# Opening of a transformer-layer kernel on one TensorE core: x in six 96-token chunks, first products by quarters

## The reference, cut to what matters

```python
u = rms_norm(h, g_mix_pre[i])                    # h is x; y = x * rsqrt(mean(x*x) + eps) * g
qa, ka, va, qb, kb, vb = jnp.split(u @ w, IN_SPLITS, axis=-1)
# then: two attention mixers per head, gates, merge, output projection,
# h + rms_norm(...), FFN with relu squared, and a gated per-layer embedding
```

## Time and profile before

| | |
|---|---|
| median of 3 runs | 1178.62 us (1177.7 to 1179.76) |
| the profiled execution: its time / its span | 1179.02 us / 1177.3 us |
| TensorE busy, share of the span | 98% |
| weight loads busy | 93% |
| VectorE, ScalarE, GpSimd busy | 41%, 36%, 43% |
| mean granted TensorE clock | 0.991 |
| chain that ended last: TensorE's share | 91% |

### The profile page before, as it was taken

One profiled execution on the slowest core, in us unless ns is written; L12 is line 12 of the kernel. 1 busy time (PEld: TensorE's weight loads), 2 busy tenths in 40 slices (PEclk: granted clock), 3 DMA queues, 4 the chain that ended last, 5 costly groups with the idle time before them and its releaser, 6 DMA issues.

```text
span 1177.3 us, 23187 instructions
## 1 busy us (share of the span) xinstructions
PE 1151.8 (98%) x8374; PEld 1094.8 (93%) x8374; DVE 487.3 (41%) x910; ACT 425.9 (36%) x905; POOL 508.6 (43%) x424
## 2 busy tenths in 40 slices
PE   8999999999999999999999989999999999999897
PEld 7888888888888889999999989999999999999897
DVE  2655555656534341112352276215413421541665
ACT  5344444454443444332233253213212221222342
POOL 3545544453444333333445454534444444444541
PEclk8999999999999999999999999999999999999899
DMA  5233422222232222232222212322222222222122
GB/s 158 82 92 93 137 75 82 89 89 69 84 93 75 92 75 63 81 101 80 81 84 86 63 54 72 99 81 82 87 81 80 80 86 84 80 80 81 53 72 81
DMA packets 167338, 98.82 MB, mean 84 GB/s; under 512 B 8801, under 2 KB 162650, under 8 KB 167282
## 3 DMA queue, kind: packets, MB, share of 16 engines
q1 hardware_dynamic: 159538, 82.05, 24.0%
q0 software_dynamic: 7744, 16.02, 4.2%
HBM read 88.57 MB, written 11.02 MB: 85 GB/s over the span
## 4 chain that ended last, share of the span: by engine, by line
PE 91%; DVE 5%; ACT 1%; issue 1%; POOL 0%; DVEq 0%; ACTq 0%
PE proj L1353 75%; PE turn_out L1525 3%; PE score L1443 3%; PE turn_out L1504 2%; PE turn_out L1520 1%; DVE wide L1219 1%; PE turn_out L1389 1%; PE turn_out L1475 1%; PE score L1450 1%; DVE hT L1248 1%; PE score L1381 1%; ACT prob L679 1%; DVE prob L1043 1%; PE turn_out L1537 1%; DVE act_lo L1237 1%
## 5 line engine op out<-in xcount | busy, mean ns | idle before, releaser
L463 POOL TENSOR_TENSOR w_lo<-w_raw,w_hi 128x512 fp32r<-128x512 f32 x292 | 394.4, 1354 | 587.8 <-ACT w_hi L627 587.6
L1353 PE MATMUL proj<-act_hi,w_hi 128*128 128x288 f32 x1600 | 362.5, 308 | 8.8 <-DVE act_lo L1237 3.5
L1353 PE MATMUL proj<-act_lo,w_hi 128*128 128x288 f32 x1600 | 344.4, 297 | 0.0
L1353 PE MATMUL proj<-act_hi,w_lo 128*128 128x288 f32 x1600 | 343.6, 297 | 0.0
L627 ACT ACTIVATE w_hi<-w_raw 128x512 fp32r<-128x512 f32 x292 | 182.3, 628 | 380.9 <-PE proj L1353 379.2
L1353 PEld LDWEIGHTS proj<-act_hi,w_hi 128*128 128x128 f32 x1600 | 255.0, 190 | 29.8 <-issue 16.6
L1353 PEld LDWEIGHTS proj<-act_lo,w_hi 128*128 128x128 f32 x1600 | 259.0, 190 | 0.0
L1353 PEld LDWEIGHTS proj<-act_hi,w_lo 128*128 128x128 f32 x1600 | 258.8, 190 | 0.0
L1353 PE MATMUL proj<-mid_hi,w_hi 128*128 128x288 f32 x640 | 137.3, 296 | 0.0
L1353 PE MATMUL proj<-mid_hi,w_lo 128*128 128x288 f32 x640 | 137.3, 295 | 0.0
L1353 PE MATMUL proj<-mid_lo,w_hi 128*128 128x288 f32 x640 | 137.3, 295 | 0.0
(11 more groups left out here) (207 smaller groups left out, 1110.7 us busy)
## 6 DMA issues: line engine op xcount, KB each, us to landing
w_raw<-w_in SPq DMA_DIRECT2D x72, 256.0 KB, 3.0
w_raw<-w_up SPq DMA_DIRECT2D x64, 256.0 KB, 2.8
w_raw<-w_down SPq DMA_DIRECT2D x64, 256.0 KB, 2.8
w_raw<-w_gate SPq DMA_DIRECT2D x32, 256.0 KB, 2.7
w_raw<-w_branch_b SPq DMA_DIRECT2D x16, 256.0 KB, 2.9
w_raw<-w_out SPq DMA_DIRECT2D x16, 256.0 KB, 2.8
w_raw<-w_ple_gate SPq DMA_DIRECT2D x16, 256.0 KB, 2.9
out<-k_tm POOLq DMA_DIRECT2D x12, 256.0 KB, 3.8
```

The costliest lines, as they stand in the source:

```text
L463: pool.tensor_tensor(w_lo[:, slot], w_raw[:, slot], w_hi[:, slot].bitcast(F32), ALU.subtract).then_inc(lo_done, 1)
L1353: last = pe.matmul(out[:, h], w[:, slot, at], x[:, k, HALF * h:HALF * h + HALF], start=(k == 0 and s == 0), stop=(k == blocks - 1 and s == 2))
```

## The change

Six chunks of 96 tokens (XC, XR) instead of 4 x 128 + 64: chunks 0 to 2 are token half 0, chunks 3 to 5 are half 1 (the last is 32 prompt and 64 sample tokens, by two DMAs). SP issues weight pieces 0 and 1 between the two triples of chunks. The 16 half-block tiles (X_TILES) are taken in four groups of four: features 0-511 of half 0, features 0-511 of half 1, then features 512-1023 of half 0 and of half 1. They rotate through four banks (score and turn_out, two halves each); proj is no longer used for x. Each tile takes three transposes, one ScalarE split (L637 after), one VectorE subtraction (L952 after) and one VectorE copy to hT (L955 after), all on 288 columns and reading the bank. Products go by groups: projection 0 for the group, then projection 1. Idle matmuls before the first products go from 16 + 40 to 8 + 4 + 16 (the last 16 on half of the array's rows each). Squares, means and roots are regrouped: one mean and one root over all six chunks instead of five each.

```diff
-        X_EARLY = 4
-        def x_bank(j):
-            return (score, turn_out, proj[0], proj[1])[j if j < X_EARLY else j % 2]
+        GROUP = KB // 2
+        X_TILES = [(GROUP * (g // 2) + j, g % 2) for g in range(4) for j in range(GROUP)]
+        def x_bank(i):
+            return (score[:, 0:HALF], score[:, 512:512 + HALF],
+                    turn_out[:, 0:HALF], turn_out[:, 512:512 + HALF])[i % GROUP]
...
-            for t in range(QB - 1):
-                sp.dma_start(x_tm[:, t], xp[P * t:P * t + P]).then_inc(x_loaded[t], 16)
-            sp.dma_start(x_tm[0:SMP, QB - 1], xs_d).then_inc(x_loaded[QB - 1], 16)
-            piece(Count(0), k_half(w_in[0], 0, b_cols[0]))
+            for c in range(XC // 2):
+                sp.dma_start(x_tm[:, c], xp[XR * c:XR * c + XR]).then_inc(x_loaded[c], 16)
+            for j in range(2):
+                piece(Count(j), k_half(w_in[0], 0, b_cols[j]))
+            for c in range(XC // 2, XC - 1):
+                sp.dma_start(x_tm[:, c], xp[XR * c:XR * c + XR]).then_inc(x_loaded[c], 16)
+            sp.dma_start(x_tm[0:XR - SMP, XC - 1], xp[SEQ - (XR - SMP):SEQ]).then_inc(x_loaded[XC - 1], 16)
+            sp.dma_start(x_tm[XR - SMP:XR, XC - 1], xs_d).then_inc(x_loaded[XC - 1], 16)
+            for j in range(2):
+                piece(Count(2 + j), k_half(w_in[0], 1, b_cols[j]))
...
-            for t in range(QB - 1):
-                root_x(t)
-            for p in range(2):
+            for p in range(RING):
                 lo_part(Count(p))
...
-            root_x(QB - 1)
...
+            pool.wait_ge(x_mean, 1)
+            pool.tensor_tensor(r_x, sq_x, neg_half[0:XR, 0:1].broadcast_to([XR, XC]), ALU.pow).then_inc(x_rooted, 1)
             for n in range(6):
                 lo_part(Count(RING + n))
...
+            def split_x(i):
+                j, h = X_TILES[i]
+                act.wait_ge(x_turned, i + 1)
+                act.activation(act_hi[:, j, HALF * h:HALF * h + HALF], x_bank(i), ACT.Copy,
+                               scale=gcol[:, G_PRE + j:G_PRE + j + 1]).then_inc(g_hi, 1)
...
+            for i, (j, h) in enumerate(X_TILES):
+                c = slice(HALF * h, HALF * h + HALF)
+                dve.wait_ge(g_hi, i + 1)
+                dve.scalar_tensor_tensor(out=act_lo[:, j, c], in0=x_bank(i), scalar=gcol[:, G_PRE + j:G_PRE + j + 1],
+                                         in1=act_hi[:, j, c].bitcast(F32), op0=ALU.mult, op1=ALU.subtract
                                              ).then_inc(g_split, 1)
+                dve.tensor_copy(hT[:, j, c], x_bank(i)).then_inc(x_kept, 1)
...
             pe.wait_ge(idle_ready, 1)
-            keep_warm(16, 512, 512)
+            keep_warm(8, 512)
...
+            for c in range(3):
+                pe.wait_ge(x_loaded[c], 16)
+                for i in range(GROUP):
+                    turn_x(i, (c,))
+                if c < 2:
+                    keep_warm(2, P)
+                else:
+                    keep_warm_halves(8, 512)
...
+            def first_products(m, group):
+                kh, h = group // 2, group % 2
+                p = 2 * kh + m
+                if h == 0:
+                    pe.wait_ge(lo_done, p + 1)
+                for j in range(GROUP):
+                    k, at = GROUP * kh + j, slice(P * j, P * j + P)
+                    pe.wait_ge(g_split, GROUP * group + j + 1)
...
+            for group in range(4):
+                for j in first_products(0, group):
+                    pass
+                if group == 0:
+                    for c in range(3):
+                        pe.wait_ge(x_loaded[3 + c], 32 if c == 2 else 16)
+                        for i in range(GROUP):
+                            turn_x(GROUP + i, (c,))
+                if group == 3:
...
+                for j in first_products(1, group):
+                    if 0 < group < 3:
+                        turn_x(GROUP * (group + 1) + j, (0, 1, 2))
```

More of the change, by code:

```diff
@@ L666, in _ @@
+            split_x(3)
+            square_x(2)
+            square_x(3)
+            for i in range(4, 8):
+                split_x(i)
+            hi_part(Count(2))
+            hi_part(Count(3))
+            square_x(4)
+            for i in range(8, 12):
+                split_x(i)
+            square_x(5)
+            hi_part(Count(RING))
+            for i in range(12, 16):
+                split_x(i)
+            hi_part(Count(RING + 1))
             act.wait_ge(lam_ready, 1)
@@ L1365, in unit_steps, with two_tasks @@
                     yield from k_steps(u * 3 + (PJ_IN + n), u * 6 + 2 * n, act_hi, act_lo)
-            def two_tasks(n, p, ready, before, between=None):
+            def two_tasks(n, p, ready, before):
                 tasks = [k_steps(Count(n + j), Count(p + j), act_hi, act_lo, apart=2) for j in range(2)]
@@ L1373, in two_tasks @@
                         next(task)
-                    if between:
-                        between(k)
             def row_matmuls(r, valid):
@@ L1383, in row_matmuls, with keep_warm, keep_warm_halves @@
                 return last
-            def keep_warm(count, first, n):
+            def keep_warm(count, n):
                 for _ in range(count):
-                    pe.matmul(turn_out[:, first:first + n], idle_w[:, :], idle_x[:, 0:n], start=True, stop=True)
+                    pe.matmul(proj[1][:, 0:n], idle_w[:, :], idle_x[:, 0:n], start=True, stop=True)
+            def keep_warm_halves(count, apart):
+                for _ in range(count):
+                    for r in range(2):
+                        rows_ = slice(64 * r, 64 * r + 64)
+                        pe.matmul(proj[1][:, apart * r:apart * r + HALF], idle_w[rows_, :], idle_x[rows_, 0:HALF],
+                                  start=True, stop=True)
@@ new lines, in turn_x @@
+            def turn_x(i, chunks):
+                j, h = X_TILES[i]
+                if i >= GROUP:
+                    pe.wait_ge(x_kept, i - GROUP + 1)
+                for c in chunks:
+                    last = pe.transpose(x_bank(i)[:, XR * c:XR * c + XR], x_tm[:, 3 * h + c, P * j:P * j + P],
+                                        ident[0:XR, 0:XR])
+                if chunks[-1] == 2:
+                    last.then_inc(x_turned, 1)
+            for c in range(3):
[6 more added lines that the diff above has]
+                    keep_warm_halves(8, 512)
@@ new lines, in _ @@
+            pe.wait_ge(gains_ready, 1)
+            def first_products(m, group):
[6 more added lines that the diff above has]
+                    pe.wait_ge(g_split, GROUP * group + j + 1)
+                    for s, (w, x) in enumerate(((w_hi, act_hi), (w_lo, act_hi), (w_hi, act_lo))):
+                        last = pe.matmul(acc[m][:, h], w[:, p, at], x[:, k, HALF * h:HALF * h + HALF],
+                                         start=(k == 0 and s == 0), stop=(k == KB - 1 and s == 2))
+                    if h == 1 and j == GROUP - 1:
+                        last.then_inc(w_used, 1)
+                    yield j
@@ L1426, in in_between @@
-                    row_matmuls(r_x, rows).then_inc(x_row_ready, 1)
-            for b in range(2):
-                pe.wait_ge(x_kept[b], 1)
-            two_tasks(PJ_IN, 0, g_split, 0, between=in_between)
+                    pe.wait_ge(x_rooted, 1)
+                    for c in range(XC):
+                        at = 512 * (c // 3) + XR * (c % 3)
+                        last = pe.matmul(score[:, at:at + XR], r_x[:, c:c + 1].broadcast_to([XR, P]),
+                                         ident[0:XR, 0:XR], start=True, stop=True)
```

117 lines of the change are left out of this document (30 added, 87 removed).

## The result

| | before | after |
|---|---|---|
| median of 10 runs each | 1178.61 us (1176.07 to 1179.76) | 1171.67 us (1168.29 to 1175.57) |
| ratio | | 0.9947 (95%: 0.9934 to 0.9959) |
| profiled execution: time, span, mean clock | 1179.02, 1177.3, 0.991 | 1171.4, 1169.8, 0.993 |
| first product | 17.65 | 11.53 |
| third projection | 39.42 | 32.46 |

The kernel became 0.5% faster: 6.9 us in the medians, 7.5 in the two spans, of which 6.96 had been won by the third projection. What stands behind it is 0.6 shorter. The forecast was 1170.9; but its two terms came out otherwise: the start 6.1 earlier instead of 7.4, and the way to the third projection 20.9 instead of 21.5.

What follows compares the result with a forecast made beforehand. TensorE, busy 98% of the span, bounds the kernel, so only the opening can yield time: -7.4 - 3.7 + 2.8 + 0.6 = -7.7 us takes the profiled 1179.0 to 1171.3, median 1170.9; range 1168.0 to 1174.5.

Steps and rivals of the forecast that it cites:

- 7.4 earlier: Opening: the first product comes at 10.2 us instead of 17.65.
- chunk 2 (1.18 MB) at 6.7 to 7.1: Opening, data stream: the last x chunk of half 0 is there at 6.7 to 7.1 us.
- The bound of 11.4: Latest first product, 11.4 us, if weight piece 0 lands only when 2.1 MB had landed before (9.39).
- at 0: Opening: TensorE's wait for half 1's x chunks, asked for at 11.9 us, costed at 0; 0.8 kept for the range.
- +2.8: First product to third projection: 16 more transposes between add 1.8 us, five more product-transpose changes at 0.2 add 1.0.
- -3.7: First product to third projection: low clock (2.8 us) and waits for w_lo and VectorE's first projection result removed.
- rival 1: Opening: the clock falls after all, costing 1.4 to 2.8 us, time 1172.3 to 1173.7; chance 0.27.
- +0.6: Groups 1 to 3: new TensorE waits for VectorE's tiles, 0.1 to 1.4 us in sum, taken as 0.6.
- rival 2: VectorE sets the pace: subtraction 0.8 us, a tile 1.3, waits 5.2 us instead of 0.6, time 1175.5; chance 0.08.
- The rule on small tiles: VectorE and ScalarE: fixed latency per instruction, tiles of 512 elements or more advised; by it 288-column tiles are wrong.
- Rival 3: Opening: the weights land late, first product at 11.4 us, time 1172.1; chance 0.10.
- rivals 4 and 5: Lead lost behind 39 us, 1178.6, chance 0.03; clock at 1.2 GHz until the third projection, 1185.2, chance 0.04.

Runs made afterwards that it cites:

- Run 9: Changed kernel with x chunks 0 to 4 loaded over all 128 partitions, a third more bytes, only 96 rows of each used: 1172.19 us, ratio 0.9954.
- run 11: Changed kernel with VectorE's hT copies behind each group's four subtractions and more idle matmuls, second run of this combination: 1170.67 us, ratio 0.994.
- Run 10: Changed kernel with copies last, more idle matmuls and x cut as 128, 128, 32 and 128, 96, 64 tokens: 1176.2 us, ratio 0.9984.
- run 1: The changed kernel measured again, unchanged: 1172.64 us, ratio 0.9957 to the kernel before.
- run 3: Changed kernel with VectorE's four copies to hT moved behind each group's four subtractions: 1170.04 us, ratio 0.9936.
- run 12: Kernel before with three x blocks transposed ahead instead of four, and 12 idle matmuls filling the stand before the first product: 1179.09 us, ratio 1.0022.
- run 2: Changed kernel with each 96-token chunk of x loaded by two transfers, of 64 and 32 rows: 1173.98 us, ratio 0.9964.
- run 4: Changed kernel with all 28 idle matmuls of the opening removed: 1171.49 us, ratio 0.9944.

## Why the prediction was right, and where its terms were off

- *The start, "7.4 earlier"*: 6.1. The rule that TensorE, ScalarE and GpSimd follow the bytes held, link for link. The term that was mis-sized is "chunk 2 (1.18 MB) at 6.7 to 7.1": it took the stream's 0.4 MB per us of before, whose chunks cover 128 partitions, for chunks of 96. Measured were 219 to 315 GB/s from 3 to 9 us, and 8.26. Run 9 shows why. The bound of 11.4 was passed by 0.13.
- *Half 1's chunks "at 0"*: the 0.62 us of waiting at 14.82, inside the 0.8 kept for the range, and from the same cause.
- *"+2.8"* for 16 more transposes and five changes: too much. A round of three products and three transposes costs 0.68 in run 11's chain, against 0.95 by the forecast's prices (3 x 0.139 + 3 x 0.11 + 0.2). Eight rounds make 2.2 us less, and two terms of the price were off. A transpose of 96 tokens takes 0.08 instead of 0.11: that is the gain that the forecast had foreseen but left unpriced (at most 1.0), some 0.7 in these rounds. The larger part, some 1.5, is the 0.2 for a change from products to transposes and back, of which next to nothing is left (3 x 0.139 + 3 x 0.083 = 0.67). The 0.2 was read from rounds with four transposes of 128 tokens and one of 64. Run 10, whose transposes are of unequal size again, pays 0.31 more a round; run 11, with three of 96, does not. Why unequal sizes cost this is not known.
- *"-3.7"*: the clock stayed at full from 6.6 us (6.5 in run 1) to past the third projection in the changed kernel's two profiles, and the waits for w_lo and vT are gone. But run 3 shows that it does not always stay up, and that a fall then costs about 0.6 rather than the 2.8 of rival 1, because it lies beside the wait for data. Rival 1 was priced too high; its other half came true as far as the idle matmuls go: the 16 on half rows took 1.32 together, two at a time.
- *"+0.6"* for VectorE: the six delays before the products at 17.84, 18.64, 22.79, 23.57, 27.67 and 28.46 (distance to the matmul before, less the 0.13 of a product) are 0.23, 0.29, 0.16, 0.28, 0.11 and 0.28, together 1.35, the top of the range given (0.1 to 1.4). Against rival 2, the subtractions took 0.51. The rule on small tiles that the forecast quoted has its price here, but a small one: two steps of half the columns are 0.79 of VectorE's time where one pair of before was 1.40 for all (0.67 + 0.73), so 0.09 more a tile.
- *Nothing behind the third projection*: 1137.3 against 1137.9, with the same low clock there in both profiles. Rival 3's late start came true in its amount (11.53 against 11.4), but with x and not the weights as the late one; rivals 4 and 5 did not.

The sum, from the forecast's -7.7 at the third projection: +1.3 for the start, +0.6 for the wait for data, -2.2 for the rounds, +0.75 for VectorE make -7.25; measured are -6.96, and 0.3 stay without a name. So the total was right within 0.8 us partly by luck: late data and VectorE's waits (+2.65) and cheap rounds (-2.2) cancelled, and neither had been foreseen in its size. What stays open: how much of the gain would remain had before kept its clock. From the trace it is 6.96 less 2.8, about 4.2, but run 12 could not show it, and before's own runs lie in two clusters, near 1176 and 1179, which may be its low clock coming and going: over the four chips the mean granted clock of the 32 runs below 1177.3 is 0.9926 and that of the 35 from 1178 on is 0.9909, which at half pace makes some 2.0 of the 2.8 us between them (an estimate: 0.0017 x 1177). Where in the span that clock was lost isn't on record; no profile of the faster cluster was taken.

## What to carry to other kernels

Before cutting the first transfers smaller, ask how many partitions each piece still covers: here 96 of 128 cost 25 to 30% of the rate (182 ns a packet against 242 to 259) exactly where everything waited for bytes. Chunks of unequal size are not the way out: run 10 won no bytes by them and paid 0.31 us in every round. And read a low clock by what waits beside it: the same 6.8 us cost 2.8 where TensorE was last and 0.6 where data was.

## What the runs showed of the hardware

- A transfer over 96 partitions is slower than one over 128. From 3 us on the 4-KB packets took 178 ns (before) and 182 (run 9) at 128 partitions, 259 at 96 (the changed kernel; 239 to 259 over all nine profiles that load the same six chunks whole), 271 with 64 and 32 (run 2). The Trainium skill, page "SBUF — State Buffer", section "Door 1: The DMA port swizzle", says that the first 64 partitions reach only half of the 16 ports and the other half serve the upper 64. An estimate from that mapping: 96 rows put 64 on eight ports and 32 on the other eight, the first eight take as long as they do for 128 rows, and the rate is three quarters of the full one. The trace agrees: 182 over 259 is 0.70, over 242 0.75. That the ports are the cause is the page's word; no run here measures a port.
- Sixteen idle matmuls of 64 rows, alternating between the row halves, took 1.32 us, 0.08 each, where one on the full array takes 0.139. The Trainium skill, page "TensorE: Matmul & The Clock Gate", Part 3, says that matmuls on different row groups overlap; the trace agrees.
- A printed clock of 1.00 at the start of a span can be the lack of a record. Products went at half pace under it until 16.9 in run 4 (12 in 3.22 us with no idle matmul ahead) and until 14.4 in run 9 (12 in 2.99, with all idle matmuls ahead). The pace of equal products is the safer witness.
- With a second wait put ahead of ScalarE's first activation, the load of its function table (1.28 us) ran behind both waits, at 5.50 instead of at 1.0 (run 10).
